# Four transpositions of the values, moved behind a small score product on TensorE

## The reference

```python
qh = rmsnorm(q.reshape(B, S, H, dh), qn_w)      # 8 heads of 64
kh = rmsnorm(k.reshape(B, S, H, dh), kn_w)
log_f = log_sigmoid(f_logit + f_bias); c = cumsum(log_f)
s = (qh @ kh^T) * scale + c_t - c_s             # only s <= t
o = softmax(s) @ vh
y = rmsnorm(o, on_w) * silu(z)
...
merged = sigmoid(g_A) * (y_a @ P_A) + sigmoid(g_B) * (y_b @ P_B)
out = rmsnorm(x + merged @ W_out, final_norm_w)
```

## Time and profile before

| | us |
|---|---|
| median of 3 runs | 942.23 |
| lowest and highest of them | 941.62, 942.93 |
| the profiled execution, its own time | 942.96 |
| its span in the trace | 941.2 |
| around the span | 1.76 |

### The profile page before, as it was taken

The page is one execution under the profiler, slowest core; times in us unless marked ns, Lnnn a source line. Parts: engine busy times, 40 slices in busy tenths (PEclk is TensorE's granted clock), DMA queues, the critical chain, the costliest instruction groups (busy, mean ns, idle before and its releaser), DMA issues.

```text
span 941.2 us, 15988 instructions
## 1 busy us (share of the span) xinstructions
PE 924.7 (98%) x6413; PEld 703.7 (75%) x6413; DVE 610.6 (65%) x984; ACT 472.6 (50%) x846; POOL 19.8 (2%) x29
## 2 busy tenths in 40 slices
PE   7999999999999999999999999999999999999997
PEld 6778787888788876676766666666667888888886
DVE  7587568799999934454486786867863524247262
ACT  7556654632866625532656547466454543334132
POOL 1000002020000000000000000000000000000000
PEclk9999999999999999999999999999999999999999
DMA  7011451249323393322553325234124332223162
GB/s 251 24 49 45 113 166 45 69 170 209 92 91 112 113 262 87 102 75 90 135 187 92 112 101 169 90 111 126 34 69 167 93 98 66 79 112 112 24 207 83
DMA packets 114576, 104.35 MB, mean 111 GB/s; under 512 B 33144, under 2 KB 94720, under 8 KB 114120
## 3 DMA queue, kind: packets, MB, share of 16 engines
q1 hardware_dynamic: 103112, 80.53, 31.1%
q10 hardware_dynamic: 10240, 18.62, 5.4%
q0 software_dynamic: 1152, 4.19, 1.4%
HBM read 76.32 MB, written 27.00 MB: 110 GB/s over the span
## 4 chain that ended last, share of the span: by engine, by line
PE 45%; DVE 3%; ACT 1%; DMA 1%; issue 1%; SPq 0%; DVEq 0%; ACTq 0%
PE pj L2296 6%; PE pj L2298 5%; PE pj L2297 5%; PE pc L2429 4%; PE pa L2395 3%; PE pa L2364 1%; PE pj L2307 1%; PE pj L2309 1%; PE pj L2308 1%; PE pb L2455 1%; PE pj L2567 1%; PE pj L2566 1%; PE pj L2565 1%; PE pb L2444 1%; DVE pa L2028 1%; PE pa L2399 1%
## 5 line engine op out<-in xcount | busy, mean ns | idle before, releaser
L147 PE MATMUL pj<-h_hi,w_hi 128*128 128x512 f32 x504 | 203.8, 404 | 0.5 <-DVE w_lo L135 0.5
L148 PE MATMUL pj<-h_lo,w_hi 128*128 128x512 f32 x504 | 196.9, 391 | 0.0
L149 PE MATMUL pj<-h_hi,w_lo 128*128 128x512 f32 x504 | 196.6, 390 | 0.0
L147 PEld LDWEIGHTS pj<-h_hi,w_hi 128*128 128x128 f32 x504 | 94.5, 188 | 23.9 <-issue 1.1
L149 PEld LDWEIGHTS pj<-h_hi,w_lo 128*128 128x128 f32 x504 | 94.6, 188 | 20.4
L148 PEld LDWEIGHTS pj<-h_lo,w_hi 128*128 128x128 f32 x504 | 94.7, 188 | 17.9 <-issue 0.2
L2296 PE MATMUL pj<-h_hi,w_hi 128*128 128x512 f32 x248 | 101.4, 409 | 0.3 <-PEq L327 0.3
L2297 PE MATMUL pj<-h_lo,w_hi 128*128 128x512 f32 x248 | 96.9, 391 | 0.0
L2298 PE MATMUL pj<-h_hi,w_lo 128*128 128x512 f32 x248 | 96.8, 390 | 0.0
L2296 PEld LDWEIGHTS pj<-h_hi,w_hi 128*128 128x128 f32 x248 | 46.5, 188 | 19.6 <-issue 10.1
L601 ACT ACTIVATE xc<-pj 128x512 f32<-128x512 f32 x39 | 23.3, 597 | 72.4 <-PE pj L149 71.8
(11 more groups left out here) (377 smaller groups left out, 1869.5 us busy)
## 6 DMA issues: line engine op xcount, KB each, us to landing
w_raw<-in_w_in SPq DMA_DIRECT2D x48, 512.0 KB, 4.4
fox_scratch<-xc ACTq DMA_DIRECT2D x39, 256.0 KB, 2.7
qkv<-in_x SPq DMA_DIRECT2D x8, 512.0 KB, 5.8
fa<-rows_scratch POOLq DMA_DIRECT2D x8, 512.0 KB, 4.8
rv<-fr_scratch SPq DMA_DIRECT2D x16, 256.0 KB, 3.9
ma<-m_scratch SPq DMA_DIRECT2D x8, 512.0 KB, 3.9
rv<-in_w_out SPq DMA_DIRECT2D x8, 512.0 KB, 3.8
w_raw<-in_x SPq DMA_DIRECT2D x8, 512.0 KB, 4.4
```

Of the source, the lines that this page charges most:

```text
L147: nc.tensor.matmul(o, w_hi[:, slot, k], h_hi[:, k, cols], start=(k == 0), stop=False)
L148: nc.tensor.matmul(o, w_hi[:, slot, k], h_lo[:, k, cols], start=False, stop=False)
L149: last = nc.tensor.matmul(o, w_lo[:, slot, k], h_hi[:, k, cols], start=False, stop=(k == KT - 1))
```

## The change

In the first key block (v = 0) of each pair, the second call of `turn_values` moves from before `max_scores(p, 5)` to behind it, directly ahead of `fill(4)`. Nothing is added or removed.

```diff
                         key_scores(p, v)
                         past_only(p, v)
-                        if v == 0:
-                            turn_values(p, 1)
-                        else:
+                        if v:
                             values(p, v - 1)
                         if v == 1 and p:
                             square_sums(p - 1, 1)
                         max_scores(p, 5 + 2 * v)
                         if v in (1, 2):
                             max_scores(p, 6 + 2 * v)
+                        if v == 0:
+                            turn_values(p, 1)
                         fill(4)
```

## The result

| | before | after |
|---|---|---|
| median, us | 942.12 (21 runs) | 943.68 (21 runs) |
| lowest to highest, us | 941.13 to 943.61 | 942.94 to 946.88 |
| ratio, 95% interval | | 1.0018 (1.0012 to 1.0024) |
| span of the profiled execution, us | 941.2 | 941.4 |

The change costs 1.56 us of the median. The two spans differ by only 0.2 us, because in this one execution what stands ahead of the attention was done 1.14 us sooner: the first maxima product of the first pair started at 473.14 us instead of 474.28. From that product to the last matmul (474.28 to 935.55 before, 473.14 to 935.75 after) it is 461.27 us before and 462.61 after, **1.34 us more**. It is from one execution of each kernel.

What follows compares the result with a forecast made beforehand. The prediction took TensorE, busy 98% of the span, as the bound, with VectorE setting the sixth product's start. Four pairs at 0.40 us gave 942.23 + 1.6 = 943.8 us, range 942.1 to 945.2 (8 times in 10).

Steps and rivals of the forecast that it cites:

- The transpositions stood in the shadow of a wait: Ahead of the sixth maxima product, the four transpositions lie wholly beside VectorE's reduction in all four pairs and cost nothing.
- The start of the sixth product does not move: The sixth maxima product waits for VectorE's row maximum, so its start relative to the work ahead moves by 0.
- The idle time of 0.7 to 1.1 us: Sign expected in the profile after: TensorE idle for 0.7 to 1.1 us before the sixth maxima product in each pair.
- 0.40 us a pair behind it: Between the sixth product and the second filling matmul, the four transpositions add 0.40 us a pair, from 0.33 to 0.44.
- the two ways of the working: Price of four transpositions: 0.44 us from eight between full-array products, 0.33 to 0.38 from their own starts.
- No later wait swallows it: Behind the fill, no later wait absorbs TensorE's delay, so four pairs pay 1.6 us; the rival that it is swallowed: 12%.
- this very sign: Third pair's sixth product: no idle time shown, but it starts 0.15 us after VectorE's end, so VectorE sets the start.
- The copy on ScalarE is covered: ScalarE's values copy comes 0.45 and 0.38 us late in pairs two and three, cost 0; rival that it is too late: 10%.
- The sum: Whole kernel: 4 x 0.40 = 1.6 us more, 943.8 us against the median of 942.23, 0.17% slower.
- rival *faster: TensorE, not VectorE, sets the sixth product's start; 1.8 us gained, 940.4 us; chance 6%.
- The 0.34 us between two filling matmuls: First two filling matmuls behind a half-array product: 0.34 us instead of 0.23, taken as the size of the mode change's drain.

Runs made afterwards that it cites:

- one_before: The kernel before with only the last of the four second transpositions in each pair, in the old place; ratio 1.0008 to the kernel before.
- two_before: The kernel before with the four second transpositions made twice over in the same place; ratio 1.0008 to the kernel before.
- mid_fill: The changed kernel with the second transpositions behind two of the four filling slices instead of ahead of them; ratio 1.0017 to the kernel before.
- slice_instead: The changed kernel with one filling slice of the first key block moved ahead of the sixth maxima product; ratio 0.9994 to the kernel before.
- one_after: The changed kernel with only the last of the four second transpositions in each pair; ratio 1.0013 to the kernel before.
- two_after: The changed kernel with the four second transpositions made twice over; ratio 1.0036 to the kernel before.
- end_fill: The changed kernel with the second transpositions behind all four filling slices; ratio 1.0031 to the kernel before.
- slice_again: The kernel before with one filling slice moved ahead of the sixth maxima product, behind the transpositions, in a second timing; ratio 0.9993 to the kernel before.

## Why the prediction was right

- **The transpositions stood in the shadow of a wait.** Right, and shown from both sides: three quarters fewer there change nothing (one_before), twice as many are paid just where the wait was short (two_before).
- **The start of the sixth product does not move.** Right. From the first to the sixth maxima product it is 10.88, 10.69, 10.18 and 10.52 us after, 10.88, 10.65, 10.18 and 10.50 before. The idle time of 0.7 to 1.1 us came out as 0.69 to 1.10.
- **0.40 us a pair behind it.** The second filling matmul comes 0.98 us behind the product in all four pairs, against 0.59 to 0.61 before: 0.37 to 0.39 more. It lies between the two ways of the working: 0.33 to 0.38 by single starts was a little low, 0.44 by the eight transpositions of the first half too high for this place. The high one counts the long step behind the first matmul that follows the transpositions (0.31 us instead of 0.23); here such a step (behind the product) stood in the fill already. In mid_fill, where it did not, the four cost the 0.44.
- **No later wait swallows it.** Wrong in the first pair. From the sixth product to the next pair's first the distances grew by 0.22, 0.34 and 0.42 us, and to the last matmul by 0.30, so 0.17 of 0.39 were lost in the first. There the eighth maxima product, in the next key block, had been set by VectorE as well, with no idle time shown. The reading that it waits for, the eighth and the ninth product, before, then after:

```profile
490.43 0.14 DVE L2028 DVE_READ_ACCUMULATOR2_ANT vecs<- 128x1 f32 x1
...
490.72 0.35 PE L2364 MATMUL pa<-qk 64*128 64x256 f32 x1
...
491.07 0.47 PE L2364 MATMUL pa<-qk 64*128 64x512 f32 x1
```

```profile
489.51 0.14 DVE L2028 DVE_READ_ACCUMULATOR2_ANT vecs<- 128x1 f32 x1
...
489.88 0.38 PE L2364 MATMUL pa<-qk 64*128 64x256 f32 x1
...
490.17 0.47 PE L2364 MATMUL pa<-qk 64*128 64x512 f32 x1
```

  Before, the eighth starts 0.15 us after the reading's end, which is the distance of a product that waits for VectorE; after, 0.23. From the sixth product to the eighth it is 5.56 us before and 5.86 after, 0.30 more and no longer 0.39; to the ninth 5.91 and 6.15, 0.24 more. So by the ninth 0.15 of the 0.17 us are gone. I had used this very sign at the sixth product of the third pair and not looked for it further on. Runs made for other ends bear it out. In slice_instead the sixth product stands where it stood (10.87 us after the first), and between it and the eighth there are the four transpositions more and one filling slice less than before, 0.31 us less in all; the seventh comes 2.89 us after the sixth instead of 3.20, but the eighth at 5.57 instead of 5.56:

```profile
490.32 0.14 DVE L2028 DVE_READ_ACCUMULATOR2_ANT vecs<- 128x1 f32 x1
...
490.61 0.35 PE L2364 MATMUL pa<-qk 64*128 64x256 f32 x1 [0.32 <-DVE vecs L2028]
```

  It waits for VectorE, so work taken out ahead of it gives nothing in this pair. The first bit put in costs nothing either: in one_after the seventh comes 0.07 us later than before, the ninth 0.01. From the seventh product to the ninth two_after, mid_fill and end_fill lose 0.13 to 0.14 us of their delay, as the changed kernel does (0.38 to 0.24).
- **The copy on ScalarE is covered.** Right, with less to spare than was worked out. It starts 1.01 us after the sixth product in the second to fourth pair, not 0.94. Against the sixth product that is 0.52, 0.45 and 0.10 us later than before, where 0.45, 0.38 and nothing were worked out; the idle time shown ahead of it is 0.41 and 0.33 us in the second and third pair. VectorE's gate product in the third pair did not wait, but of the 0.17 us that were to be left ahead of it 0.09 were: the sigmoid, which started at 608.09 and took 0.63, ended at 608.72, and the product started at 608.81. end_fill shows what the loss of that cover costs, about 1.1 us in the third pair.
- **The sum.** 4 x 0.40 = 1.6 us was forecast; the medians give 1.56, the stretch 1.34. The ratio's interval, 1.0012 to 1.0024, stands for 1.1 to 2.3 us and holds both sides of the 0.2% that I had set as the bound of what can be told. That the medians come within 0.04 us of the forecast is therefore partly luck. The stretch is 0.26 us short of it, mostly by the 0.17 of the first pair and by 0.08 of the fourth, whose 0.38 us are 0.30 at the last matmul; where those 0.08 went is not shown.
- The rival *faster* needed a sixth product set by TensorE. In two_before, where that is so in the second and third pair, the distance to VectorE's reading is 0.34 and 0.41 us, not 0.15. The Trainium skill (TensorEngine Tiling (Array Packing), Key Properties) says that changing the tiling mode drains TensorE. These traces agree in kind: the half-array product of two_before starts 0.20 us after the last of its transpositions (544.72 + 1.09 - 0.27 = 545.54 to 545.74), where one transposition follows another after 0.12. The 0.34 us between two filling matmuls, by which the prediction had put a size to it, don't show it: both use the full array, and behind transpositions, with no change of mode, that step is 0.31 us too. The changed order has two changes of mode fewer, and gains nothing by it, since they lay in the wait.

## What to carry to other kernels

A queue that waits for another engine has a pocket of free time just ahead of the waiting instruction. What is moved from before it to behind it is paid for, however small it is (here 0.37 to 0.39 us for four transpositions whose record is 0.66 us long), unless a later wait of the same queue takes it up, as one did with part of it in the first pair. The distance from the releaser's end to the start (here 0.14 to 0.15 us) tells better whether a product waits than the idle time shown, which can be zero when the work ahead just fills the pocket. Fill the pocket up with work that no one waits for. In slice_again the sixth product came 0.12 to 0.52 us later than before and the trace still gained; how much more would hold up the next engine's queue was not tried.

## What the runs showed beyond that

- The time at which the second half began, far ahead of the change, lay between 472.90 and 475.26 us in the eleven profiled executions. That is more than the effect, so spans of single executions could not be compared; stretches between two products could, to some 0.05 us where nothing between them had been changed, except where a load came late (1.0 us in one of eleven). Only one kernel was profiled twice.
- A transposition of 128 by 128 costs TensorE 0.10 to 0.11 us where nothing covers it: 1.14 us for twelve (one_after against after), 1.74 for sixteen (two_after against after).
